# Second mixer of a two-layer encoder: the triple mixtures on VectorE are issued after the low parts instead of before them

## The reference, cut to what matters

```
hp = pad(h, one token on each side)
xx = 0.5 * (hp[:, :-2] + hp[:, 2:]) - h
xr, xw, xk, xv, xa, xg = (h + xx * mu[i] for i in range(6))
r, k, v = xr @ w_r, xk @ w_k, xv @ w_v            # three 1024 x 1024 products
g  = sigmoid(xg @ g1) @ g2                        # low rank, 160
lw = tanh(xw @ w1[z]) @ w2[z]                     # low rank, 64, two directions z
la = (xa @ a1[z]) @ a2[z]                         # low rank, 64, two directions z
```

## Time and profile before

| what | value |
|---|---|
| median of 3 runs | 1340.69 us (1339.78 to 1341.02) |
| profiled execution, its own time | 1336.92 us |
| span of the profiled execution | 1335.0 us |
| PE busy in the span | 95% |
| DVE, ACT, POOL busy | 71%, 48%, 33% |
| granted PE clock, mean | 0.976 of full speed |

### The profile page before, as it was taken

One profiled execution on the slowest core, in us unless ns is written; L12 is line 12 of the kernel. 1 busy time (PEld: TensorE's weight loads), 2 busy tenths in 40 slices (PEclk: granted clock), 3 DMA queues, 4 the chain that ended last, 5 costly groups with the idle time before them and its releaser, 6 DMA issues.

```text
span 1335.0 us, 30542 instructions
## 1 busy us (share of the span) xinstructions
PE 1268.5 (95%) x12736; PEld 1146.1 (86%) x12736; DVE 942.4 (71%) x1334; ACT 644.5 (48%) x1045; POOL 435.1 (33%) x220
## 2 busy tenths in 40 slices
PE   7999999999899999899998699899999999899998
PEld 5899999878789999799998698898888887799998
DVE  7666667786776776877676995766666656877765
ACT  5544446462644444644445367433333333544453
POOL 1244442211144444344443000443333412244442
PEclk9999999999999999999999799879999999999999
DMA  8355554323345545455455253010000013455543
GB/s 336 142 186 181 182 182 175 132 95 142 142 176 183 184 183 210 160 186 184 184 189 199 97 184 137 2 50 3 4 3 3 4 50 106 188 189 185 186 185 126
DMA packets 18667, 188.18 MB, mean 141 GB/s; under 512 B 2064, under 2 KB 2576, under 8 KB 3600
## 3 DMA queue, kind: packets, MB, share of 16 engines
q1 hardware_dynamic: 18576, 186.84, 38.2%
HBM read 185.78 MB, written 1.05 MB: 140 GB/s over the span
## 4 chain that ended last, share of the span: by engine, by line
PE 79%; DVE 14%; ACT 4%; issue 2%; DMA 0%; SPq 0%; DVEq 0%; ACTq 0%
PE gu_bank L257 22%; PE gu_bank L259 11%; PE bank L1381 7%; PE bank L236 7%; PE bank L237 7%; PE bank L238 7%; PE gu_bank L1400 4%; PE gu_bank L236 3%; PE gu_bank L238 2%; PE gu_bank L237 2%; DVE WL L193 2%; PE gu_bank L1381 2%; ACT WH L186 1%; DVE XSQ L407 1%; DVE HX L383 1%
## 5 line engine op out<-in xcount | busy, mean ns | idle before, releaser
L202 POOL TENSOR_TENSOR WL<-raw,WH 128x1024 fp32r<-128x1024 f32 x102 | 341.5, 3349 | 598.0 <-ACT WH L187 576.9
L257 PE MATMUL gu_bank<-HX,WH 128*128 128x512 f32 x1408 | 506.8, 402 | 14.6 <-DVE WL L193 11.8
L259 PE MATMUL gu_bank<-HX,WL 128*128 128x256 f32 x1408 | 396.8, 282 | 0.0
L193 DVE TENSOR_TENSOR WL<-raw,WH 128x2048 fp32r<-128x2048 f32 (+1 forms) x114 | 252.5, 2215 | 137.8 <-ACT WH L186 137.7
L257 PEld LDWEIGHTS gu_bank<-HX,WH 128*128 128x128 f32 x1408 | 266.7, 189 | 80.0 <-DVE WL L193 9.2
L259 PEld LDWEIGHTS gu_bank<-HX,WL 128*128 128x128 f32 x1408 | 268.0, 190 | 0.2
L186 ACT ACTIVATE WH<-raw 128x2048 fp32r<-128x2048 f32 (+1 forms) x114 | 204.6, 1794 | 22.9 <-PE gu_bank L238 13.5
L236 PE MATMUL bank<-PH,WH 128*128 128x256 f32 (+1 forms) x720 | 201.7, 284 | 1.0 <-ACT arena L1921 1.0
L237 PE MATMUL bank<-PL,WH 128*128 128x256 f32 (+1 forms) x720 | 201.6, 283 | 0.0
L238 PE MATMUL bank<-PH,WL 128*128 128x256 f32 (+1 forms) x720 | 201.5, 283 | 0.0
L438 ACT ACTIVATE work<-work 128x256 f32<-128x256 f32 x88 | 36.8, 418 | 303.2 <-DVE work L490 303.2
(11 more groups left out here) (307 smaller groups left out, 2027.2 us busy)
## 6 DMA issues: line engine op xcount, KB each, us to landing
raw<-stream_in SPq DMA_DIRECT2D x114, 1536.0 KB, 6.6
cst<-const_in SPq DMA_DIRECT2D x1, 1568.0 KB, 16.6
X<-xT_in SPq DMA_DIRECT2D x1, 1024.0 KB, 4.8
raw<-stream_in SPq DMA_DIRECT2D x1, 1024.0 KB, 6.9
arena<-hconst_in SPq DMA_DIRECT2D x2, 512.0 KB, 10.3
out<-X SPq DMA_DIRECT2D x4, 256.0 KB, 2.3
arena<-hconst_in SPq DMA_DIRECT2D x1, 768.0 KB, 13.4
arena<-fw_in SPq DMA_DIRECT2D x1, 512.0 KB, 7.7
```

Source lines behind the costliest of these rows:

```text
L193: nc.vector.tensor_tensor(WL[:, slot, :cut], raw[:, slot, :cut], WH[:, slot, :cut].bitcast(fp32), ALU.subtract).then_inc(lo_ready, 1)
L202: (eng or nc.gpsimd).tensor_tensor(WL[:, slot, cut:end], raw[:, slot, cut:end], WH[:, slot, cut:end].bitcast(fp32), ALU.subtract).then_inc ...
L257: nc.tensor.matmul(out[:, :], WH[:, slot, w:w + P], HX[:, x, :, :].rearrange("p i t -> p (i t)"), start=k == 0, stop=False)
L259: return nc.tensor.matmul(out[:, L:2 * L], WL[:, slot, w:w + P], HH[:, x, :], start=False, stop=k == CT - 1)
```

## The change

In the loop over windows, the triple mixtures of windows 2 to 5 are issued after the window's low parts (of weights, single mixtures, triple mixtures) and no longer ahead of its single mixtures. The instructions themselves, their operands and their semaphores are the same.

```
             for n in range(2, RKV_STEPS):
-                if n < 6:
-                    for j in (2 * n - 4, 2 * n - 3):
-                        mix_triple(j)
                 for i in WINDOW[n]:
                     mix(i)
                 if n == 7:
...
                 low(n)
                 for i in WINDOW[n]:
                     lo(i)
                 if 3 <= n < 7:
                     for j in (2 * n - 6, 2 * n - 5):
                         lo_triple(j)
+                if n < 6:
+                    for j in (2 * n - 4, 2 * n - 3):
+                        mix_triple(j)
                 if n == 6:
                     dve.wait_ge(kk_ss, 1)
                     ts(KSQ[0:16, 0, :], KB[2][0:16, 0:L], 1e-24, None, ALU.max).then_inc(kk_max, 1)
```

## The result

| | before | after |
|---|---|---|
| median, 8 runs each | 1340.65 us (1338.66 to 1342.46) | 1334.64 us (1328.61 to 1337.55) |
| ratio after to before | | 0.9949, 95% interval 0.9932 to 0.9966 |
| profiled execution (its span) | 1336.92 us (1335.0) | 1337.55 us (1335.6) |

The change saves 6.0 us by the medians. The profiled execution of the changed kernel is the slowest of its eight, and its span is even 0.6 us longer than the span profiled of the kernel before. So one pair of traces can't show the gain as a whole; it can show the stretches.

What follows compares the result with a forecast made beforehand. The prediction took PE's chain of waits as the bound, with PE stopped 4.59 us at k6 for DVE's queue. Terms of -2.38 and -0.43 us summed to -2.81 us: 1340.69 to 1337.9 us, range 1335.6 to 1340.1.

Steps and rivals of the forecast that it cites:

- Term 1: Before block k6 in the second mixer: DVE's queue loses window 2's triple mixtures, shortening PE's stop to 2.21 us; -2.38 us.
- Term 2: PE's clock behind the k6 stop: 3.4 us at the low level, loss 1.49 in place of 1.92 us; -0.43 us.
- the rival that the clock holds: At k6, the shorter stop costs no fall of the clock; gain 4.30 us, 1336.4 us; chance 0.22.
- Windows 3 to 5: Claimed DVE keeps up with the earlier PE: no new stop, no price; tightest slack, at r5, 2.1 us.
- The chain carries the shift to the end: Behind the windows, later stops follow PE's blocks, so the whole 2.81 us saved reaches the program's end.
- the sum as the difference of the medians: Whole kernel: the -2.81 us counted on the profiled execution was taken from the median, 1340.69 to 1337.9 us.
- the low clock did not last as long as before: Rival behind k6: the low clock lasts 6.8 us again; Term 2 +1.0, gain 1.4 us, 1339.3; class chance 0.16.
- DVE did not become the bound: Rival at r5, or r3 before it: DVE's windows hold PE up; slower, 1345.6 us in full form; chance 0.05.
- the change did what it says: Its opposite was the rival: something else releases k6 at the old time, no effect, 1340.7 us; chance 0.04.
- a later stretch that changes through its own clock: Rival: a later stretch of the program gives back a microsecond; classed with the long low clock, together chance 0.16.

## Why the prediction was wrong

**Term 1, the queue ahead of k6: right.** A stop of 4.5 to 4.7 us became one of 1.95 to 2.32 us in the seven traces; I had 2.21. The instructions moved along as counted, and no other input of k6 was late. (What the prediction calls six triple mixtures ahead of k6 are six instructions, which make two of them.)

**Term 2, the clock behind the stop: right in size.** I had 3.4 us at the low level after the restart; six of the seven traces have 3.4 and one has 3.1. In six the fall came between 0.3 us before the restart and 0.05 us after it, close to what I had assumed, and in the first 0.6 us after it. Both terms together were 2.81 us and measured 2.84. All seven traces, with stops of 1.95 to 2.32 us, show the fall, and the rival that the clock holds falls with that. The Trainium skill's page "TensorE: Matmul & The Clock Gate", section "Why this matters for your kernels", warns only of gaps above about 3 us; the traces do not agree with it, and the measurement decides.

**Windows 3 to 5: right.** No new stop, and the two halves of the change show the slack as counted. Without the moves in windows 3 to 5, the low part for r5 comes no sooner, so its slack of 2.5 us less the 2.81 us by which PE comes sooner is short by 0.3 us, and window 2 alone shows a stop of 0.25 us there, of 0.4 us lost in the opening. In that run's expectation I had it larger.

**"The chain carries the shift to the end", and the sum as the difference of the medians: this is the step that failed.** I took the time behind the windows to be the same in both kernels, but for chance. It is not. The traces of before lose 2.6 us more between x0 and the scan in every execution, and those of after in one of seven, which makes 2.25 us on the mean. Behind k6 the clock's falls are not chance against PE's work: in each of the seven traces with a distance of 50.1 to 50.3 us the next one stands 21.4 to 21.6 us behind the start of x0. The fall near 842 us stands in the first trace of before too; I had let the clock behind the opening be, but for a microsecond that a rival gave back. With 2.84 + 2.25 us and 0.56 us behind the scan the traces place 5.65 us of a gain of 6.0 and 6.65 us by the two pairs of medians. That takes the traced executions for a fair sample of all: had none of the seven traces been at 50.2 us, the 2.25 us would be 2.6, and with two of them 1.9. The 0.56 us are less than the spread of that stretch from trace to trace (475.7 to 482.3 us in both kernels together), so neither they nor the last 0.35 to 1.0 us are placed with certainty.

The rivals: the clock did not hold; the low clock did not last as long as before; DVE did not become the bound; the change did what it says. None of them held the true case, which was a gain of the forecast's mechanism with a second one behind it. The nearest, a later stretch that changes through its own clock, had the sign the other way: it gave a microsecond back. My range allowed 0.8 us for the runs' spread on the low side, taken from three runs of before. The changed kernel's spread is 9 us, from 1328.6 to 1337.6.

## What to carry to other kernels

Look in a hand-ordered queue for what stands ahead of the entry that another engine waits for, and move what has slack behind it; count the slack of each later window before you do. In this kernel PE's clock fell at its stops, and 2 us less in one stop moved the moment at which all later work met the clock. This was worth nearly as much as the stop itself (2.25 us beside 2.84), and it can go the other way: with k6's inputs first, 0.6 to 1.1 us were lost again in the same stretch. In such a case a single pair of traces misleads, and stretches cut at fixed instructions over several traces tell more than spans.

## What was unexpected of the hardware

A stop of 1.95 us of PE was enough for a fall of its clock, and in that trace the fall came 0.6 us after PE was at work again; without a stop there the clock did not fall, in two traces. Executions of the kernel before vary by 0.12 us in the opening over five traces, and by 0.01 us from x0 to the scan, while from the scan to the end they vary by over 5 us (476.9 to 482.3). Added work of 0.7 us on PE's path shortened the next stretch by 2.6 us, in one trace. And 1.9 us taken off the path in the opening, by what k6 needs going first, left the median where it was (1334.2 and 1333.5 against 1334.6 and 1334.1 us).
